# Attention stages of a fused four-layer kernel: all four first roundings put behind the copies of the turned probabilities, and the gate's product ahead of the softmax's last step

## What is computed

```
h = rms_norm(x, g) @ w_in
o_a = causal attention, 8 heads, keys of 128 + 64 (rope)      # even layer
o_b = causal attention, 8 heads of 128 (the selection of blocks keeps all at this length)
o_m = attention over 256 memory rows, 4 heads of 128
y = concat([o_a, o_b, o_m]) * silu(gate);  x = x + y @ w_out
# odd layer: 16 sliding-window heads of 64 with a sink each, 6 dilated heads of 128, 4 memory heads
```

## Time and profile before

| | |
|---|---|
| median of 3 runs | 2272.14 us |
| the profiled execution | 2272.14 us, its span 2270.3 us |
| TensorE matmul busy | 2174.3 us, 96% |
| GpSimd busy | 1783.4 us, 79% |
| ScalarE busy | 1254.7 us, 55% |
| VectorE busy | 1206.4 us, 53% |
| mean granted TensorE clock | 0.987 |

### The profile page before, as it was taken

One profiled execution on the slowest core, in us unless ns is written; L12 is line 12 of the kernel. 1 busy time (PEld: TensorE's weight loads), 2 busy tenths in 40 slices (PEclk: granted clock), 3 DMA queues, 4 the chain that ended last, 5 costly groups with the idle time before them and its releaser, 6 DMA issues.

```text
span 2270.3 us, 38561 instructions
## 1 busy us (share of the span) xinstructions
PE 2174.3 (96%) x12244; PEld 1873.7 (83%) x12244; DVE 1206.4 (53%) x1893; ACT 1254.7 (55%) x2249; POOL 1783.4 (79%) x1401
## 2 busy tenths in 40 slices
PE   8999999999999999989998899999999999999997
PEld 6887888888888887888886778888888888877886
DVE  6456775255661277732566644544644664378612
ACT  6475466565555465555664345445655544467654
POOL 7788687988989876789887747786799887756795
PEclk9999999999999999999999999999999999999998
DMA  7565435666667544456665434554466656533464
GB/s 255 179 182 169 125 108 160 187 185 185 187 195 211 179 131 129 126 167 189 183 203 160 150 103 152 175 181 151 139 203 190 195 184 181 185 116 116 140 187 134
DMA packets 211827, 379.05 MB, mean 167 GB/s; under 512 B 23648, under 2 KB 34528, under 8 KB 211552
## 3 DMA queue, kind: packets, MB, share of 16 engines
q1 hardware_dynamic: 207360, 369.52, 53.8%
q10 hardware_dynamic: 4320, 7.66, 1.0%
HBM read 374.99 MB, written 2.10 MB: 166 GB/s over the span
## 4 chain that ended last, share of the span: by engine, by line
PE 52%; POOL 26%; issue 13%; DVE 6%; ACT 2%; POOLq 1%; DVEq 0%; ACTq 0%
PE ps L517 31%; POOL w_lo L438 26%; PE ps L518 16%; PE ps L785 1%; PE ps L636 1%; DVE sm L2184 1%; PE ps L807 1%; DVE ps L1523 1%; DVE tb L1522 1%; POOLq L437 0%; DVE w L1528 0%; PE ps L761 0%; ACT w_hi L894 0%; PE ps L797 0%; PE ps L547 0%
## 5 line engine op out<-in xcount | busy, mean ns | idle before, releaser
L438 POOL TENSOR_TENSOR w_lo<-raw,w_hi 128x512 fp32r<-128x512 f32 (+1 forms) x1386 | 1768.3, 1295 | 465.4 <-ACT w_hi L894 419.9
L894 ACT ACTIVATE w_hi<-raw 128x512 fp32r<-128x512 f32 (+1 forms) x1420 | 863.2, 618 | 763.8 <-PE ps L518 684.3
L517 PE MATMUL ps<-xa,w_hi 128*128 128x512 f32 x2832 | 1015.0, 402 | 23.4 <-POOL w_lo L438 11.6
L518 PE MATMUL ps<-xa,w_lo 128*128 128x256 f32 x2832 | 794.3, 280 | 0.0
L517 PE MATMUL ps<-xb,w_hi 128*128 128x512 f32 x2160 | 762.9, 398 | 3.7 <-POOL w_lo L438 1.8
L517 PEld LDWEIGHTS ps<-xa,w_hi 128*128 128x128 f32 x2832 | 536.0, 189 | 155.6 <-POOL w_lo L438 15.4
L518 PE MATMUL ps<-xb,w_lo 128*128 128x256 f32 x2160 | 602.9, 279 | 0.0
L518 PEld LDWEIGHTS ps<-xa,w_lo 128*128 128x128 f32 x2832 | 538.6, 190 | 0.9
L517 PEld LDWEIGHTS ps<-xb,w_hi 128*128 128x128 f32 x2160 | 405.3, 188 | 101.5 <-POOL w_lo L438 3.0
L518 PEld LDWEIGHTS ps<-xb,w_lo 128*128 128x128 f32 x2160 | 407.1, 188 | 0.6
L1522 DVE TENSOR_SCALAR tb<-ps 128x512 f32<-128x512 f32 (+1 forms) x120 | 82.4, 687 | 323.2 <-PE ps L518 321.8
(11 more groups left out here) (330 smaller groups left out, 2111.8 us busy)
## 6 DMA issues: line engine op xcount, KB each, us to landing
raw<-w_gate_dram SPq DMA_DIRECT2D x128, 256.0 KB, 3.0
raw<-w_ogz_dram SPq DMA_DIRECT2D x128, 256.0 KB, 3.0
raw<-w_odin_dram SPq DMA_DIRECT2D x128, 256.0 KB, 3.0
raw<-w_evmoba_dram SPq DMA_DIRECT2D x112, 256.0 KB, 3.0
raw<-w_ein_dram SPq DMA_DIRECT2D x96, 256.0 KB, 3.2
raw<-w_evout_dram SPq DMA_DIRECT2D x80, 256.0 KB, 3.0
raw<-w_odgate_dram SPq DMA_DIRECT2D x72, 256.0 KB, 2.8
raw<-w_einz_dram SPq DMA_DIRECT2D x64, 256.0 KB, 2.9
```

Source lines behind the costliest of these rows:

```text
L438: nc.gpsimd.tensor_tensor(w_lo[:, slot, 0:n], raw[:, at, 0:n], w_hi[:, slot, 0:n].bitcast(F32), SUB).then_inc(lo_pool, 1)
L517: mm(ps[:, bank + b, :], w_hi[:, slot, at], x[:, x0 + k, :], start=(k == 0), stop=False)
L518: ins = mm(ps[:, bank + b, 0:T], w_lo[:, slot, at], x[:, x0 + k, 0:T], start=False, stop=(k == st.blocks - 1))
L894: af(w_hi[:, slot, 0:n], raw[:, at, 0:n], ACT.Copy).then_inc(act_rounded, 1)
```

## The change

On ScalarE, for couple c, the copies of the turned probabilities stood between the roundings of units 0, 1 and those of units 2, 3 of the next chunk; now they stand ahead of all four. After the last couple of a stage the four roundings are those of the next stage. On VectorE, `gate_out` of couple c stood behind `softmax_out` of couple c+1 and now stands ahead of it.

```diff
@@ scalar engine, attend
                 for c, heads in enumerate(couples):
                     p, _, last = gate_chunk(couples, c)
-                    for start, end in ((0, 2), (2, 4)):
-                        if c + 1 < len(couples):
-                            chunk(c + 1, start, end)
-                        else:
-                            for q in range(start, end):
-                                rounded(ST[then], 0, q)
-                        if start == 0:
-                            turned_copy(heads, a + 2 * c)
+                    turned_copy(heads, a + 2 * c)
+                    if c + 1 < len(couples):
+                        chunk(c + 1, 0, 4)
+                    else:
+                        for q in range(4):
+                            rounded(ST[then], 0, q)
                     if last == st.upp:
@@ vector engine, attend
                     keep(heads, a + 2 * c)
-                    if c + 1 < len(couples):
-                        softmax_out(couples[c + 1], a + 2 * c + 2)
                     if last == st.upp:
                         dve.wait_ge(at_done, a + 2 * c + 2)
                         gate_out(st, p, heads[-1]["gate"], x_at + 2 * p, x_count + p + 1)
+                    if c + 1 < len(couples):
+                        softmax_out(couples[c + 1], a + 2 * c + 2)
```

## The result

The changed kernel is slower: 2289.85 us against 2276.2 (medians of 7 runs), ratio 1.0058 with a 95% interval of 1.0037 to 1.008, or +13 us (8 to 18). A second measurement gave 1.0058 again (1.0042 to 1.0074). The forecast was +6.75 us, on a kernel before that then stood at 2272.14, and a range of 2274.0 to 2284.5, that is +1.9 to +12.4: the direction was right, the size half of what was measured.

The account below looks back on a forecast made before the run. TensorE, busy 96%, was taken to bound the kernel, except in half couples, where the softmax chain outlasts the matmuls. Terms 2.25 + 1.0 + 0.4 + 3.9 - 0.8 = +6.75 us on 2272.14 gave 2278.9, range 2274.0 to 2284.5.

Parts of the forecast that it names:

- Full couples and ends of stages: TensorE's first unit waits for GpSimd's low half: 2.25 us at stage ends, 0.2 in each of five full couples, 1.0.
- ScalarE's lateness: Full couples: two more roundings ahead of the sigmoid delay no later unit; taken as 0, upper bound 2 us.
- The leg after an even couple: Half (sliding-window) couples: second turn to next second turn, no gate between, takes 9.2 us, set by TensorE's units.
- The entry: Start of the half couples: the 1.42 us wait loses its 1.07 block, the late first unit returns 0.3: -0.8 us.
- The leg after an odd couple: Half couples: second turn to next second turn, with the gate's product on the chain, takes 11.35 us.
- The 4.4 above: Softmax's first step and keeping of outputs after odd half couples: 4.4 us, including one 0.55 us hold-up by GpSimd.
- The clock: Half couples: TensorE's clock likely drops once per period of two couples, costing 0.8 us a period.
- Part two: VectorE's gate product ahead of the softmax's last step: 0 in full couples, 2.9 us on the chain in half couples.
- Faster: Half couples: VectorE's hold-ups by GpSimd vanish and nothing takes their place; -7.9 us, 2264.2; chance 0.04.
- Worse: L2170 is blocked twice in half couples (12.6 us) and unit 5 is late in five couples; +12.4, 2284.5; chance 0.15.
- Same: Half couples: the clock holds and one L2170 slips between two GpSimd operations; +2.55 us, 2274.7; chance 0.24.

Follow-up runs that it names:

- part two alone: Kernel before with only VectorE's gate product moved ahead of the softmax's last step, roundings as before: ratio 1.0026, half couples 94.7 us.
- part one alone: Kernel before with only ScalarE's four roundings put behind the copies, gate product left where it was: ratio 1.0009, half couples 82.6 us.
- the last two kernels with the old orders: Kernel before with maximum and exponentials in PSUM, then also the sink's exponential, both orders as before: ratios 0.997 and 0.9959.

## Why the prediction missed

- **Full couples and ends of stages** (forecast 2.25 + 1.0): the mechanism held; the size was too small. GpSimd's end to TensorE's start takes 0.16 us (1598.22 + 1.27 to 1599.65), where I had put 0.05. Ends: 1.07, 0.8 and 0.8, together 2.7. In full couples the first unit comes 0.35 us later in each of the five places, where I had put 0.2. Full couples, means of two profiles each: +1.1 in the second stage and +1.0 in the third, 2.1 together, of which some 0.4 is the part that part two alone shows too. Sum 4.7 against 3.25. ScalarE's lateness was put at 0, and no unit behind the first came late.
- **The leg after an even couple** was right: 9.3 against 9.2, with the first unit 0.85 to 1.05 late.
- **The entry** was right: the wait of 1.42 fell to 0.39, -1.0 against the forecast's -0.8.
- **The leg after an odd couple** is the step that failed: "The 4.4 above holds one block of 0.55." Both L2170 were blocked, 1.8 us in all, so 4.4 was 5.6 and the leg 12.3, as in the case I had set apart with a chance of 0.15 ("a second up to 12.6"). GpSimd's four operations follow each other without a gap, and VectorE has two operations that need the port in that time; the prediction took over the one block seen before without counting which of the two would meet which of the four. Three such legs are +3 against the sum. The kernel with the maximum in PSUM shows it: no block, and the leg is 10.5, where the prediction had "None would give 10.8". The half couples as a whole came out at +5.3 (means of two profiles each) against a forecast of 3.9 + 0.4 - 0.8 = 3.5.
- **The clock** (forecast +0.8 a period): one drop in the second period and one in the third, none in the first; the second profile of the changed kernel has one in each of the three. Over the stretch 0.06 x 91.6 = 5.5 us were lost against 0.04 x 85.2 = 3.4 before, but the second profile of the kernel before lost 0.06 x 86.6 = 5.2, so these profiles do not fix the size of this term. It hung on the block: with waits of 0.8 us the clock stayed at 1.00. The prediction has a drop cost nothing before "where VectorE was the limit"; behind the last half couple that limit ends, and there a drop in the kernel before cost 1.4 us: 15.4 us from 2085.05 to the next first turn in its second profile, 14.0 from 2075.20 in the first.
- **Part two.** It was costed as one step on the chain, and is by far the dearer part: alone +8 to +9.5 us in the half couples, where part one alone gave back 3 to 4. About 2.5 us of the product's 2.9 came on top of each odd leg, and the even legs, which were to fall by as much as 1.3, did not.
- **The rivals.** "Faster" named a real gain. It is to be had by moving data and not the order: ratio 0.9959, some 9 us, against the 7.9 it gave. "Worse", at +12.4, is the nearest to the +13 measured, by half of its mechanism: L2170 was blocked twice, but unit 5 came late in no full couple, so that its number fits so well is luck. "Same" needed a free L2170 and a clock that holds, and neither came.

**What stays open.** The profiles add up to about +10 us (half couples 91.2 - 85.9 = 5.3, the rest 4.7), the timed runs say 13, with the lower end of the second interval at 9.6. Some 1.3 us more lie behind the attention stages, where nothing was changed either: from the third stage's next unit to the end of the span it is 118.3 and 118.4 us in the two profiles of the kernel before, and 119.2 and 120.1 in those of the changed kernel. All five profiles with four late roundings at the stages' ends have 119.2 to 120.2 there, and seven of the other eight 118.3 to 118.4; the eighth, of the kernel with maximum and exponentials in PSUM, has 120.3, so the link is not shown. The parts alone, 1.0009 and 1.0026, add up to 1.0035, whereas their stretches add up to those of the whole; with the intervals as they are, this may be noise. Whether the rest is the clock's behaviour in other executions was not settled.

## What to carry to other kernels

Holding work back until after a wait moves it into the time in which the released engine needs it: look at who waits for the first of the pieces held, and leave that one ahead. Where a fast small operation is blocked by a long one of another engine, try another source for it (here PSUM, 9 us gained) ahead of another place in the order (here 13 us lost). Before costing "one block", count the operations that can be blocked against the time in which the blocker runs without a gap.

## What was not expected of the hardware

An addition of 128x2 with both operands in SBUF took 1.28 us in place of 0.16 under GpSimd's subtraction (part two alone); between the last two kernels with the old orders, the mean of 16 fell from 428 to 154 ns with one operand in PSUM. A tensor-by-scalar of 128x2 was held for up to 1.1 us beyond its 0.23 in the changed kernel and not at all with its source in PSUM (0.22 us in all 16). The Trainium skill, page "SBUF — State Buffer", section "Who interferes with whom", states both: an operation with two SBUF inputs contends with a GpSimd operation that reads SBUF, and one in a two-port mode with any. The runs agree; that the tensor-by-scalar is in such a mode is read from its being held, and no run shows it by another way. The way to the first scores took 1315.3 us in one profile of the kernel before and 1326.3 in another.
